# Probabilities times values in fp32r high and low parts: v after k and q, masks on GpSimd, a unit every 2.6 slots

## The reference, cut to what matters

```python
z = rmsnorm(x, g_norm) @ w_in              # q, k, v, attention gate, conv B, C, h, conv gate
q = rope(q); k = rope(k)
s = einsum('bnqhgd,bnkhd->bnhgqk', qb, kk) * SCALE      # 128 queries x 256 keys
s = where((diff >= 0) & (diff < WINDOW) & ..., s, NEG)  # diff = 128 + qi - kj, WINDOW = 128
p = e / (sum(e) + exp(sink - m))                        # e = exp(s - m)
o = einsum('bnhgqk,bnkhd->bnqhgd', p, vv)
mix = concat([o * silu(ga), bg * conv3(cg * hc) * silu(gc)])
x = x + mix @ w_out
x = x + sigmoid(x @ w_pg) * (p_i @ w_pp)
```

## Time and profile before

| what | value |
|---|---|
| median of three runs | 1226.89 us (1225.06 to 1227.0) |
| the profiled execution's span, first to last instruction | 1226.8 us |
| PE busy | 1187.1 us, 97% |
| DVE busy | 739.2 us, 60% |
| ACT busy | 424.5 us, 35% |
| POOL busy | 319.0 us, 26% |
| PE's waits for a division (L959), all in attention | 17.4 us, in 6 waits |

### The profile page before, as it was taken

The page is one execution under the profiler, slowest core; times in us unless marked ns, Lnnn a source line. Parts: engine busy times, 40 slices in busy tenths (PEclk is TensorE's granted clock), DMA queues, the critical chain, the costliest instruction groups (busy, mean ns, idle before and its releaser), DMA issues.

```text
span 1226.8 us, 18225 instructions
## 1 busy us (share of the span) xinstructions
PE 1187.1 (97%) x7302; PEld 1129.9 (92%) x7302; DVE 739.2 (60%) x1286; ACT 424.5 (35%) x919; POOL 319.0 (26%) x149
## 2 busy tenths in 40 slices
PE   5999899999999999999999989999999999999997
PEld 5999888888899999999999988887889999999997
DVE  2356879798535444466623587988945454444554
ACT  5311545445233222333321044454522332223333
POOL 2324321222222221221322432222122312221110
PEclk9999899999999999999999999999999999999998
DMA  7533101110121122111053311110111122121103
GB/s 210 147 84 87 34 21 32 35 35 20 41 44 58 52 53 61 43 44 53 26 155 88 87 36 35 35 31 28 30 35 35 42 69 69 41 65 44 44 1 142
DMA packets 127946, 70.40 MB, mean 57 GB/s; under 512 B 43156, under 2 KB 123860, under 8 KB 127832
## 3 DMA queue, kind: packets, MB, share of 16 engines
q1 hardware_dynamic: 122400, 61.33, 17.6%
q10 hardware_dynamic: 5464, 7.92, 2.6%
HBM read 59.10 MB, written 6.76 MB: 54 GB/s over the span
## 4 chain that ended last, share of the span: by engine, by line
PE 83%; DVE 12%; ACT 2%; DMA 1%; issue 1%; ACTq 0%; DVEq 0%
PE ring L399 73%; PE aux L422 2%; DVE yc L1063 2%; PE aux L455 2%; DVE up L1059 2%; PE aux L444 1%; PE aux L457 1%; DVE yc L1061 1%; DMA xnat<-in_x_prompt_dram 1%; DVE st L953 1%; PE aux L430 1%; DVE comb L1032 1%; DVE st L1034 1%; DVE tmp L983 0%; ACT comb L757 0%
## 5 line engine op out<-in xcount | busy, mean ns | idle before, releaser
L399 PE MATMUL ring<-act,ws 128*128 128x352 f32 x6048 | 995.6, 324 | 0.5 <-DVE rot L978 0.3
L399 PEld LDWEIGHTS ring<-act,ws 128*128 128x128 f32 x6048 | 974.1, 189 | 1.6 <-DVE act L891 0.5
L375 POOL TENSOR_TENSOR ws<-stage,ws 128x1024 fp32r<-128x1024 f32 (+1 forms) x84 | 212.0, 2524 | 841.5 <-ACT ws L629 841.5
L638 ACT ACTIVATE act<-tmp 128x352 fp32r<-128x352 f32 x120 | 59.6, 497 | 278.2 <-DVE tmp L1097 143.6
L629 ACT ACTIVATE ws<-stage 128x1024 fp32r<-128x1024 f32 (+1 forms) x84 | 91.5, 1089 | 110.5 <-issue 61.3
L371 POOL TENSOR_TENSOR stage<-stage,gT 128x1024 f32<-128x1024 f32 x52 | 107.3, 2064 | 24.3 <-DMA stage<-in_w_in_dram 13.4
L884 DVE TENSOR_TENSOR act<-tmp,act 128x352 fp32r<-128x352 f32 x120 | 73.6, 614 | 60.3 <-ACT act L638 59.5
L1117 DVE TENSOR_TENSOR tmp<-ring,gate 128x352 f32<-128x352 f32 x48 | 25.2, 524 | 75.0 <-ACT gate L816 75.0
L1095 DVE TENSOR_TENSOR tmp<-ring,act 128x352 f32<-128x352 f32 x48 | 25.2, 524 | 63.4 <-PE ring L399 63.4
L757 ACT ACTIVATE comb<-comb,st 128x128 f32<-128x128 f32 x128 | 49.9, 391 | 32.0 <-DVE st L1040 31.9
L722 ACT ACTIVATE gate<-gate 128x352 f32<-128x352 f32 x48 | 23.8, 496 | 101.8 <-DVE gate L985 76.3
(11 more groups left out here) (167 smaller groups left out, 930.0 us busy)
## 6 DMA issues: line engine op xcount, KB each, us to landing
stage<-in_w_in_dram SPq DMA_DIRECT2D x36, 512.0 KB, 3.9
stage<-in_w_in_dram SPq DMA_DIRECT2D x32, 256.0 KB, 3.8
stage<-in_w_pg_dram SPq DMA_DIRECT2D x16, 512.0 KB, 3.8
rot<-raw ACTq DMA_DIRECT2D x32, 132.0 KB, 2.3
stage<-in_w_out_dram SPq DMA_DIRECT2D x32, 128.0 KB, 2.8
stage<-in_w_out_dram SPq DMA_DIRECT2D x16, 256.0 KB, 3.1
out_dram<-xnat SPq DMA_DIRECT2D x8, 512.0 KB, 2.9
xnat<-in_x_prompt_dram SPq DMA_DIRECT2D x4, 512.0 KB, 7.1
```

Source lines behind the costliest of these rows:

```text
L375: nc.gpsimd.tensor_tensor(ws[:, s, 1, 0:n, :], stage[:, s, 0:n, :], ws[:, s, 0, 0:n, :].bitcast(F32), ALU.subtract).then_inc(w_lo, 1)
L399: mm = nc.tensor.matmul(out, ws[:, w % 2, wp, kw, :], x[:, xp, kx, cs], start=(i == 0 and wp == 0 and xp == 0), stop=(i == n - 1 and wp == 1))
L638: nc.scalar.activation(dst, tmp[:, s % 2, :], ACT.Copy).then_inc(S["hi_out"], 1)
```

## The change

- v's weight tile is taken after k and q (slots 15 to 17); its transposes go from slot 5 to slot 18 and read `vraw`, which shares memory with `up`. k and q, their rope and its DMAs come earlier by 3 slots.
- v is kept as fp32r high and low parts next to each other, 64 + 64 columns for a head group (`vsa`, `vsb`), written by ACT and DVE.
- The turned probabilities are split, high by ACT and low by DVE (`probs_low`), to `pw`; GpSimd masks the split tile (`mask`): two affine_selects, each over 128 x 1024, one for the own keys and one for the previous. Units 0 and 1 have no previous block and no mask.
- The product is then four fp32r matmuls of 512 columns (two for units 0 and 1) with 128 stationary columns. High and low v give separate halves of PSUM's partitions: ACT copies one half to the other's partitions (`ot`), and DVE adds them (`take_o`). DVE's L1048 and L1052 and ACT's L746 go.
- Unit u starts in slot 25 + floor(2.6 u): 25, 27, 30, 32, 35, 38, 40, 43, 45, 48, 51, 53, 56, 58, 61, 64. The steps: split at -2, scores at 0, division at +2 (at +1 before), turn at +2, low part and mask at +3, product at +4, sum of the halves at +5. Two buffers hold the probabilities (`comb` and half of `ptcp`).
- The two decode units come first, in slots 19 to 26. The tail's slot goes from 67 to 70.
- GpSimd's loop over weight tiles is written out, and the masks stand in it at fixed places: those of a tile's first slot between the low part of the next tile and the scaling of the one after, the others behind that scaling.

```diff
-    A_TILES = [("v", 0, C_V), ("k", 0, C_K)] + [("q", t, C_Q) for t in range(4)]
+    A_TILES = [("k", 0, C_K)] + [("q", t, C_Q) for t in range(4)] + [("v", 0, C_V)]
...
-    BCAST, V_TURN, KC_TURN, SC_TURN, QPACK = (3, 2), 5, 7, 8, 21
-    AT0 = 24
-    D0 = AT0 + 4 * NB + 2
-    TAILS = 67
+    BCAST, KC_TURN, SC_TURN, QPACK, V_TURN = (3, 2), 7, 8, 17, 18
+    D0, AT0 = 19, 25
+    TAILS = 70
...
+    def start_of(u):
+        return AT0 + 13 * u // 5
...
+            def mask(l, u):
+                n = l * (2 * NB - 2) + u - 2
+                halves = pw[1 - l % 2]
+                pool.wait_ge(S["pl_done"], l * 2 * NB + u + 1)
+                pool.affine_select(out=halves[:, 0], in_=halves[:, 1], compare_op=ALU.is_ge, fill=0.0, base=0,
+                                   pattern=[[0, 8], [1, P]], channel_multiplier=-1).then_inc(S["masked"], 1)
+                pool.wait_ge(S["masked"], 2 * n + 1)
+                pool.affine_select(out=halves[:, 1], in_=halves[:, 1], compare_op=ALU.is_gt, fill=0.0, base=0,
+                                   pattern=[[0, 8], [-1, P]], channel_multiplier=1).then_inc(S["masked"], 1)
...
+            def masks(l, f, parts):
+                for part in parts:
+                    for u in at_slot(NCH * (f - 2) + part, split=3):
+                        if u >= 2:
+                            mask(l, u)
...
+                    masks(l, f, (0,))
+                    pool.wait_ge(loaded[s], loaded_count(w))
+                    if f < NA:
+                        nc.gpsimd.tensor_tensor(stage[:, s, 0:n, :], stage[:, s, 0:n, :],
+                                                gT[:, l, :].rearrange("p (k a) -> p k a", a=1).to_broadcast([P, n, P]),
+                                                ALU.mult).then_inc(w_scaled, 1)
+                    masks(l, f, (1, 2))
+                    pool.wait_ge(w_hi, w + 1)
+                    nc.gpsimd.tensor_tensor(ws[:, s, 1, 0:n, :], stage[:, s, 0:n, :],
+                                            ws[:, s, 0, 0:n, :].bitcast(F32), ALU.subtract).then_inc(w_lo, 1)
...
+            def pv(l, u):
...
+                for which in range(1 if b == 0 else 2):
+                    for part in range(2):
+                        mm = nc.tensor.matmul(pO, v_of(m, b - which, g),
+                                              pw[m][:, which, 4 * part:4 * part + 4, :].rearrange("p a n -> p (a n)"),
+                                              start=(which == 0 and part == 0), stop=(part == 1 and which == (b > 0)))
...
+                    for u in at_slot(s, pv=4):
+                        sc.wait_ge(S["pv_done"], count(l, u) + 1)
+                        nc.scalar.activation(ot[own, :], pO[other, :], ACT.Copy).then_inc(S["o_shifted"], 1)
+                    for u in at_slot(s, turn=2):
+                        sc.wait_ge(S["p_turned"], count(l, u) + 1)
+                        nc.scalar.activation(dst, pT1, ACT.Copy).then_inc(S["ph_done"], 1)
...
                 for s in range(A_SLOTS):
-                    for step, u in units_at(s, split_last=True):
-                        if step == "norm":
-                            divide(l, u)
+                    for u in at_slot(s, norm=2):
+                        divide(l, u)
+                    for u in at_slot(s, o=5):
+                        take_o(l, u)
+                    for u in at_slot(s, low=3):
+                        probs_low(l, u)
                     behind(s)
```

More of the change, by code:

```diff
@@ new lines, in scores @@
+                n = l * 2 * NB + u + 1
+                pe.wait_ge(S["scores_taken"], count(l, u))
+                pe.wait_ge(S["qk_hi"], 3 * n)
+                pe.wait_ge(S["qk_lo"], 3 * n)
+                keys = slice(0, P if b == 0 else 2 * P)
+                for t in range(G):
+                    for part in range(2):
+                        mm = nc.tensor.matmul(pS4[:, t, keys], qst[:, g, t, :], kst[:, g, part, keys],
+                                              start=(part == 0), stop=(part == 1))
@@ new lines, in decode_cache @@
+            def decode_cache(l, g):
+                rows = slice(g * HD, (g + 1) * HD)
+                mx = 1 - l % 2
+                pe.wait_ge(S["q_packed"], l + 1)
+                pe.wait_ge(S["kc_taken"], l + 1)
+                pe.wait_ge(S["v_taken"], 2 * (l + 1))
+                pe.wait_ge(S["v_lo"], 2 * (l + 1))
+                pe.wait_ge(S["scores_taken"], l * NU + g)
+                for i in range(DB):
+                    mm = nc.tensor.matmul(pS[:, i * G * DS:(i + 1) * G * DS], kcT[mx][rows, i, :],
+                                          qps[mx][rows, i, :, :].rearrange("p a b -> p (a b)"), start=True, stop=True)
+                mm.then_inc(S["dcache_done"], 1)
@@ new lines, in _ @@
+                    for u in at_slot(s, pv=4):
+                        gg = u % 2
+                        own, other = slice(gg * HD, (gg + 1) * HD), slice((1 - gg) * HD, (2 - gg) * HD)
+                        sc.wait_ge(S["pv_done"], count(l, u) + 1)
+                        nc.scalar.activation(ot[own, :], pO[other, :], ACT.Copy).then_inc(S["o_shifted"], 1)
+                    for u in at_slot(s, turn=2):
+                        sc.wait_ge(S["p_turned"], count(l, u) + 1)
+                        sc.wait_ge(S["pv_done"], count(l, u))
+                        dst = pw[m][:, 0 if u < 2 else 1, 0:4, :].rearrange("p a n -> p (a n)")
+                        nc.scalar.activation(dst, pT1, ACT.Copy).then_inc(S["ph_done"], 1)
@@ new lines, in _ @@
+                    for u in at_slot(s, scores=0):
+                        sc.wait_ge(S["negm_done"], 2 * (count(l, u) + 1))
+                        cb = combs[u % 2]
+                        for t in range(4):
+                            nc.scalar.activation(cb[:, t, :], cb[:, t, :], ACT.Exp, bias=st[:, 1, t:t + 1],
+                                                 scale=SCALE, accum_out=st[:, 4, t:t + 1]).then_inc(S["exp_done"], 1)
+                        nc.scalar.activation(st[:, 3, :], st[:, 2, :], ACT.Exp).then_inc(S["exp_done"], 1)
@@ L765, in _ @@
+                    for gg in decode_at(s, 0):
+                        sc.wait_ge(S["dcache_done"], 2 * l + gg + 1)
+                        nc.scalar.activation(skt, pS[:, 0:P], ACT.Copy).then_inc(S["dcache_taken"], 1)
                     if kind == "bg":
@@ L1054, in _ @@
+                    for u in at_slot(s, split=-2):
+                        split_low(l, u)
                     if kind == "hc":
```

462 lines of the change are left out of this document (224 added, 238 removed).

## The result

| | kernel before | changed kernel |
|---|---|---|
| median, side by side on one chip | 1226.34 us (1225.06 to 1227.0, 4 runs) | 1287.74 us (1286.78 to 1289.37, 4 runs) |
| ratio to before, 95% interval | | 1.0508 (1.0493 to 1.0523) |
| span of the profiled execution | 1226.8 us | 1285.0 us |
| mean granted clock of TensorE | 0.986 | 0.963 |
| PE's waits in attention | 17.4 us in 6 | 81.5 us in 31 |

The change makes the kernel 5.1% slower. The forecast was 1263 us, with 1207 to 1300 as its range.

What follows compares the result with a forecast made beforehand. The prediction took PE to be the bound, with DVE next. From 1226.8 us it took 29.1 of product gain and 27.0 of old waits, leaving 1170.7, then added 70 of waits and 22 of clock: 1263 us, range 1207 to 1300.

Steps and rivals of the forecast that it cites:

- The product's gain, term 29.1: On PE, fp32r products at 0.225 us a matmul replace the fp32 products and save 29.1 us.
- the base of 1170.7: Whole kernel: 1226.8 us less 29.1 of product gain and 27.0 of old PE waits with their lowered clock.
- the rival of fp32r as slow as fp32: PE's 512-column fp32r products take fp32's time: +29 us, 1292; part of the over-1290 case, chance 0.12.
- The ledger of places, term 70: PE's new attention waits, added slot by slot for division and masks: 35 us a layer, 70 us in all.
- the ledger's ends: Attention waits a layer: low ends sum to 20.7 us, high ends, with POOL and DVE blocking each other, to 50.
- The masks, 1.65 us: On POOL, each affine_select over 1024 elements takes 1.65 us, so a unit's masks take 3.3 us.
- The estimate of 1.54 us: One POOL mask, from the skill's 1.8 cycles at 1.2 GHz for an element: 1.54 us.
- POOL and DVE hold each other up: In attention, DVE gets one instruction through between two of POOL; masks block like low parts, making the ledger's high ends.
- The clock, term 22: PE's lowered clock behind 7 waits a layer, at 1.6 us each: 22 us.
- rival 1: Attention waits of PE merge as one wait lets the other engines catch up: 1208 us; under 1222, chance 0.22.
- Rival 2: POOL's masks don't hold DVE up in attention; only the unavoidable order of steps remains: 1222 to 1235, chance 0.11.
- rival 3: POOL is the bound in attention, with masks of 2.34 us: 1302 us; over 1290, chance 0.12.

Runs made afterwards that it cites:

- e1_div1: Changed kernel with DVE's division back at start + 1, a slot behind the scores: 1249.27 us, ratio 1.0189.
- b1_div2: Kernel before with only the division moved from start + 1 to start + 2: 1239.51 us, ratio 1.0113.
- e9_tiny5: Changed kernel with division at start + 1, early masks, ACT's split first, and masks over only 8 elements: 1199.90 us, ratio 0.9781.
- e2_tiny: Changed kernel with masks over 8 elements instead of 1024, most masking left out: 1272.74 us, ratio 1.0380.
- e5_all: Changed kernel with division at start + 1, first-slot masks ahead of POOL's low part, ACT's split first in its slot: 1228.31 us, ratio 1.0013.
- e6_div1mask: Changed kernel with division at start + 1 and first-slot masks ahead of POOL's low part: 1235.32 us, ratio 1.0065.
- e4_mask: Changed kernel with the masks of a weight tile's first slot ahead of POOL's low part: 1282.71 us, ratio 1.0464.

## Why the prediction was right in kind, and where its size was off

**Direction and mechanism: right.** The forecast said that 29 us come off PE and that more than this comes back as waits, first of all of the turn for the division. That is what the rows show, and e1_div1 confirms the cause, though b1_div2 shows that the division's place is worth this much only in the changed kernel. The time fell into the forecast's own range of 1235 to 1290, at its upper end: 1287.7 against 1263. The profile's 1285.0 is 22.3 us above the sum of 1262.7, and the terms account for it: waits +11.5 in attention, waits of decode +2.1, clock +8.7. The terms that were estimates, the waits and the clock, were both low; within the waits only the masks' length was too high.

**The product's gain, term 29.1: right.** 0.23 us for a matmul against 0.225. With it the base of 1170.7 holds (e9_tiny5: 1170.5), so the rival of fp32r as slow as fp32 is out.

**The ledger of places, term 70: right in the places, 11.5 low in the sum.** PE's waits in layer 0, by slot, against the ledger's ends:

| slot | ledger | measured |
|---|---|---|
| 34 (product and turn) | 3.9 to 9 | 2.81 + 3.89 = 6.7 |
| 37 | 4.7 to 6 | 5.55 |
| 42 | 0 to 4.5 | 2.3 |
| 47, 50 | 2.2 to 5, 2.1 to 4.7 | 3.0, 3.2 |
| 53, 55 | 0 to 0.9, 3.5 to 7.2 | 0.4, 4.8 |
| 58 | 0 to 2.5 | 2.9 |
| 60, 63 | 2.2 to 5, 2.1 to 4.7 | 6.2, 5.6 |
| 27, 29, 40 | not listed | 0.5, 1.1, 0.3 |

I took the middle between "POOL never in the way" and "POOL always". Up to slot 55 that was fair: the middles make 26.9 us, the waits 25.9. What failed is the last three places, 8.3 against 14.7 us and each above its high end, and three that the ledger left out (1.9 us). DVE's slots there are not held up once but several times. This is slot 59, DVE and POOL, ahead of the wait of slot 60:

```profile
342.55 1.09 POOL L376 TENSOR_SCALAR_AFFINE_SELECT pw<-pw 128x1024 fp32r<-128x1024 f32 x1 [9.82 <-DVE pw L1071]
343.71 1.42 POOL L379 TENSOR_SCALAR_AFFINE_SELECT pw<-pw 128x1024 fp32r<-128x1024 f32 x1
344.21 3.44 DVE L1063 TENSOR_TENSOR kst<-kT,kst 64x128 fp32r<-64x128 f32 x2
345.11 2.40 POOL L401 TENSOR_TENSOR ws<-stage,ws 128x1024 fp32r<-128x1024 f32 x1
...
347.46 1.94 POOL L396 TENSOR_TENSOR stage<-stage,gT 128x1024 f32<-128x1024 f32 x1
347.68 2.08 DVE L1153 TENSOR_TENSOR up<-tmp,yc 128x320 f32<-128x320 f32 x1
...
352.55 1.11 PE L440 MATMUL aux<-ident,ptcp 128*128 128x128 f32 x4 [6.17 <-DVE ptcp L1011]
```

Masks, low part and scaling stand in a row on POOL. DVE's two small splits take 3.44 us where they take 0.60 alone, and the taps' first step 2.08 for 0.49. That is 4.4 us of delay in one slot, against the 2.8 between the ledger's two ends. The ledger had each DVE slot meet POOL about once.

The masks are not what does it here. In e2_tiny, where they take 0.23 us each, the same splits meet the low part and the scaling, and the wait is nearly as long:

```profile
339.30 2.38 POOL L401 TENSOR_TENSOR ws<-stage,ws 128x1024 fp32r<-128x1024 f32 x1 [0.56 <-ACT ws L681]
339.31 4.42 DVE L1063 TENSOR_TENSOR kst<-kT,kst 64x128 fp32r<-64x128 f32 x2
...
347.04 1.11 PE L440 MATMUL aux<-ident,ptcp 128*128 128x128 f32 x4 [5.64 <-DVE ptcp L1011]
```

Between the scores of unit 61 and the wait of slot 63 in the changed kernel no mask runs at all. The low part and the scaling (POOL, from 369.77 to 374.24) hold up the division's own steps, which take 0.16 and 0.69 us alone:

```profile
370.22 2.18 DVE L1009 TENSOR_TENSOR st<-st 128x4 f32<-128x4 f32 x1
...
372.65 2.13 DVE L1011 TENSOR_TENSOR comb<-comb,st 128x512 f32<-128x512 f32 x1
```

That is 3.5 us of delay, and with the ledger's low end of 2.1 us for this slot it makes the 5.6 measured; the high end had 2.6 for it. At both places POOL's old work on the weights, met more than once, is what the ledger had too small.

**The masks, 1.65 us: too long.** A mask takes 1.09 us when it is undisturbed (1.22 and 1.14 in the mean), so 2.2 for a unit, not 3.3. By the same ledger the waits should then have been lower than forecast, and weren't: at the last places POOL's work on the weights cost more than the shorter masks gave back. The estimate of 1.54 us from the Trainium skill (GPSIMD Engine Reference, § 3.1) was too long as well; the trace has 1.09.

```profile
L376 POOL TENSOR_SCALAR_AFFINE_SELECT pw<-pw 128x1024 fp32r<-128x1024 f32 x28 | 34.3, 1223 | 98.6 <-DVE pw L1071 98.6
L379 POOL TENSOR_SCALAR_AFFINE_SELECT pw<-pw 128x1024 fp32r<-128x1024 f32 x28 | 31.9, 1139 | 1.9
```

**POOL and DVE hold each other up: right, and now with a row for a mask.** In slot 33 of the changed kernel the split meets the low part and the masks:

```profile
181.39 2.26 DVE L1060 TENSOR_TENSOR qst<-raw,qst 64x512 fp32r<-64x512 f32 x1 [1.64 <-ACT kst L804]
183.69 2.22 DVE L1063 TENSOR_TENSOR kst<-kT,kst 64x128 fp32r<-64x128 f32 x2
185.94 2.11 DVE L1153 TENSOR_TENSOR up<-tmp,yc 128x352 f32<-128x352 f32 x1
```

```profile
180.72 2.39 POOL L401 TENSOR_TENSOR ws<-stage,ws 128x1024 fp32r<-128x1024 f32 x1 [13.32 <-ACT ws L681]
183.06 1.55 POOL L376 TENSOR_SCALAR_AFFINE_SELECT pw<-pw 128x1024 fp32r<-128x1024 f32 x1
184.68 1.09 POOL L379 TENSOR_SCALAR_AFFINE_SELECT pw<-pw 128x1024 fp32r<-128x1024 f32 x1
185.73 1.93 POOL L396 TENSOR_TENSOR stage<-stage,gT 128x1024 f32<-128x1024 f32 x1
```

The DVE rows end just behind POOL rows: L1060 at 183.65, where POOL's low part ended at 183.11; L1063's pair at 185.91, where the masks ended at 184.61 and 185.77; L1153 at 188.05, where the scaling ended at 187.66. In these rows DVE gets one instruction through between two of POOL, masks included. L1060's mean went from 686 ns to 1005. The Trainium skill (SBUF — State Buffer, § Who interferes with whom) names two SBUF inputs on DVE against a GpSimd instruction that reads SBUF as such a pair; the trace agrees, with 2.2 us for the 0.60 of L1063's pair, and DVE's 24.5 us between e5_all and e9_tiny5.

**The clock, term 22: 8.7 low.** I had 14 waits at 1.6 us. There were 31 in attention and 2 in decode, with 30.7 us in all, or 0.9 each. The places were more in number and each cost less. In the table the clock term grows roughly with the waits, but their sum doesn't fix it: e1_div1 and e6_div1mask have 52.7 and 51.2 us of waits, and 19.8 and 11.7 us of clock. What sets the term was not found out.

**Rivals.** Waits did merge (rival 1), but in the experiments, not in the changed kernel: e4_mask took 11.2 us of waits from the products and got 12.2 back at the turns. Rival 2's time, 1222 to 1235, is reached by e5_all (1228.3) and just missed by e6_div1mask (1235.3), but with another order and not by its mechanism: there POOL does hold DVE up. POOL as the bound (rival 3) doesn't hold in the changed kernel: it is busy for 75.5 of 210 us. It hurts by its place and by what it does to DVE.
